# Step sizes in four column strips among the convolution tiles, running sums spread from rows by row halves, a gate tile ahead of turning x, and a provisional mean

## What is computed

```python
xbc = silu(causal_depthwise_conv(xbc, conv_w, conv_b))      # x, B and C of the state space
xs, bm, cm = split(xbc, [D_SSM, D_SSM + GROUPS * STATE])
dt = softplus(dt_raw + dt_bias)                             # step sizes: 512 tokens x 16 heads
a = -exp(a_log)
# in chunks of 128 tokens (4 chunks), adt = dt * a:
a_cs = cumsum(adt)                                          # running sums
decay = exp(segsum(adt))                                    # exp(a_cs[l] - a_cs[s]) for s <= l
cb = einsum('bclgn,bcsgn->bcgls', cc, bc)
y_diag = einsum('bcgjls,bcsgjp->bclgjp', cb * decay, x * dt)
states = einsum('bcsgn,bcsgjp->bcgjpn', bc, x * dt * decay_to_end)
y = y_diag + y_off + d_skip * x                             # y_off from the state of the chunk before
y_ssm = rms_norm(y * silu(z_ssm), ssm_norm_g)
out = concatenate([y_att, y_ssm]) @ w_out
x = layer_norm(alpha * x + out, ln_g, ln_b)                 # mean, variance, scale, bias
```

## Time and profile before

| what | us |
|---|---|
| median of 3 runs | 1355.4 (1354.19 to 1357.29) |
| the profiled execution | 1354.75 |
| its span, first to last instruction | 1353.0 |
| TensorE busy | 1254.0 (93%) |
| VectorE busy | 625.0 (46%) |
| ScalarE busy | 461.8 (34%) |
| GpSimd busy | 158.7 (12%) |

### The profile page before, as it was taken

One profiled execution on the slowest core, in us unless ns is written; L12 is line 12 of the kernel. 1 busy time (PEld: TensorE's weight loads), 2 busy tenths in 40 slices (PEclk: granted clock), 3 DMA queues, 4 the chain that ended last, 5 costly groups with the idle time before them and its releaser, 6 DMA issues.

```text
span 1353.0 us, 17766 instructions
## 1 busy us (share of the span) xinstructions
PE 1254.0 (93%) x6976; PEld 891.0 (66%) x6976; DVE 625.0 (46%) x1131; ACT 461.8 (34%) x837; POOL 158.7 (12%) x126
## 2 busy tenths in 40 slices
PE   4899989999999889999889699999999999999996
PEld 1667556678887564454444278897556898787883
DVE  1654465554444353311111365324655745858544
ACT  3333236542222321111111251125564345555314
POOL 0200010000000000000000201602402056422000
PEclk9899999999999999999999799999999989999998
DMA  9565251023334369999999913321002312112301
GB/s 352 210 208 190 75 222 68 1 63 93 94 97 152 153 264 392 412 411 412 411 412 409 376 47 93 94 78 63 1 2 65 102 37 63 47 52 89 94 16 62
DMA packets 61633, 219.37 MB, mean 162 GB/s; under 512 B 6368, under 2 KB 6760, under 8 KB 61552
## 3 DMA queue, kind: packets, MB, share of 16 engines
q1 hardware_dynamic: 55440, 198.86, 40.3%
q10 hardware_dynamic: 3664, 10.47, 2.0%
q0 software_dynamic: 2448, 8.91, 1.7%
HBM read 203.52 MB, written 14.70 MB: 161 GB/s over the span
## 4 chain that ended last, share of the span: by engine, by line
PE 78%; DMA 8%; DVE 4%; ACT 4%; issue 4%; POOL 1%; SPq 0%; ACTq 0%; DVEq 0%; POOLq 0%
PE ps L639 12%; PE ps L640 12%; PE ps L641 12%; PE ps L926 6%; PE ps L907 4%; PE ps L735 3%; PE ps L947 3%; PE ps L758 3%; PE ps L745 3%; DMA ring<-in_w_moe 2%; PE ps L680 2%; PE ps L682 2%; PE ps L681 2%; PE ps L706 1%; DMA RG<-expert_rows,small 1%
## 5 line engine op out<-in xcount | busy, mean ns | idle before, releaser
L1615 DVE TENSOR_TENSOR ring_r<-ring,ring_r 128x1024 fp32r<-128x1024 f32 x115 | 145.8, 1271 | 206.3 <-ACT ring_r L1273 205.6
L1273 ACT ACTIVATE ring_r<-ring 128x1024 fp32r<-128x1024 f32 x116 | 121.2, 1053 | 204.4 <-PE ps L641 166.8
L639 PE MATMUL ps<-RB_r,ring_r 128*128 128x512 f32 x320 | 126.9, 396 | 1.1 <-DVE RH L1661 1.1
L641 PE MATMUL ps<-RB_r,ring_r 128*128 128x512 f32 x320 | 124.6, 389 | 0.0
L639 PE MATMUL ps<-RC_r,ring_r 128*128 128x512 f32 x224 | 91.2, 407 | 5.7 <-POOL RD_r L2380 4.7
L640 PE MATMUL ps<-RD_r,ring_r 128*128 128x512 f32 x224 | 88.0, 393 | 0.0
L641 PE MATMUL ps<-RC_r,ring_r 128*128 128x512 f32 x224 | 87.9, 392 | 0.0
L640 PE MATMUL ps<-RG_r,ring_r 128*128 128x512 f32 x208 | 81.1, 390 | 0.0
L926 PE MATMUL ps<-ring,RH 128*64 128x512 f32 x320 | 71.9, 594 | 0.0
L639 PEld LDWEIGHTS ps<-RB_r,ring_r 128*128 128x128 f32 x320 | 60.1, 188 | 16.7 <-issue 4.5
L907 PE MATMUL ps<-RD_r,RC_r 128*128 128x256 f32 x288 | 69.1, 296 | 1.2 <-DVE RD_r L1884 1.2
(11 more groups left out here) (438 smaller groups left out, 2620.3 us busy)
## 6 DMA issues: line engine op xcount, KB each, us to landing
ring<-in_w_moe SPq DMA_DIRECT2D x120, 512.0 KB, 15.6
ring<-in_w_post SPq DMA_DIRECT2D x68, 512.0 KB, 3.6
ring<-in_w_pre SPq DMA_DIRECT2D x48, 512.0 KB, 3.6
RE<-in_w_moe SPq DMA_DIRECT2D x44, 512.0 KB, 15.9
RF<-in_w_moe SPq DMA_DIRECT2D x40, 512.0 KB, 14.7
ring<-in_w_pre SPq DMA_DIRECT2D x16, 1024.0 KB, 7.0
expert_rows<-RD ACTq DMA_DIRECT2D x15, 512.0 KB, 6.9
ring<-in_w_pre SPq DMA_DIRECT2D x3, 2048.0 KB, 16.9
```

Source lines behind the costliest of these rows:

```text
L639: mm(out, part(m)[:, w], xh(k), start=first and k == 0, stop=False)
L641: ins = mm(out, remainder(m)[:, w], xh(k), start=False, stop=last and k == n_k - 1)
L1273: A(part(m), tile, ACT.Copy).then_inc(w_hi, 1)
L1615: v.tensor_tensor(remainder(m), arrival(m)[2], part(m).bitcast(F32), ALU.subtract).then_inc(w_split, 1)
```

## The change

- Step sizes: between convolution tiles 6 and 7, eight matmuls with 32 columns of weights (16 of `wdt`, 16 of zeros, copied into `cpad` during the expert stage) over 512 tokens of RA, in four column strips of one bank; ScalarE copies the bank out; before tile 8 four matmuls with `strip_sum` (16 columns that add the four strips) turn them to tokens. VectorE's and ScalarE's softplus stand in the convolution loop, at i = 9 and 11, and i = 10.
- Gate tile 0 runs directly behind the convolution tiles (bank number `PE_Z0`; the numbers behind it shift by one, so the banks' parities swap), then x is turned.
- Running sums: one matmul for sums, one for totals, two that write the sums as rows (head and chunk on partitions, twice), copied to `cs_rows`. `spread_sums` picks a row with a column of `ident` repeated 128 times, over 64 partitions, alternating between the lower and the upper half and between ps[2] and ps[3]; the semaphore comes once for both.
- GpSimd does skip product and scaling of one chunk ahead of the loop and of the next one at the end of each round.
- The end: a provisional mean from six tiles, summed by TensorE ahead of the last output tile; seven tiles are centred by it while that tile runs; squares go to RB and GpSimd adds seven of them; the mean of what is left, d, is subtracted from eight tiles (six on VectorE, two on GpSimd) and d squared from the variance.

Context lines are left out of the diff, as are renamed semaphores and lines that only moved:

```diff
@@ -205,6 +206,8 @@
+        cs_rows = w_r[:, :, :].rearrange("p k n -> p (k n)")[:, 0:P]
+        adt_all = MASK[:, 192:256]
@@ -614,7 +620,8 @@
-                        pe.wait_ge(ev[e % 2], PE_XT // 2)
+                        b = e - PE_XT - 6
+                        pe.wait_ge(ev[b], (PE_XT + 1 - b) // 2)
@@ -1039,8 +1046,23 @@
+                if i == 7:
+                    for k in range(KT):
+                        g = k % 4
+                        last = mm(ps[0][32 * g:32 * g + 32, :], cpad[:, k, :], xT(k), start=(k < 4), stop=(k >= 4))
+                    last.then_inc(heads_full, 1)
+                if i == 8:
+                    pe.wait_ge(heads_sb, 2)
+                    for t in range(TT):
+                        last = mm(ps[1][:, t * 16:t * 16 + 16], PTB[:, 0, t * P:(t + 1) * P], strip_sum, start=True, stop=True)
+                    last.then_inc(heads_full, 1)
...
+            def gate_tile(i):
+                split_column(z_tile(i), M_Z + i, two(RCr, RDr))
+            gate_tile(0)
+            pe.wait_ge(sp1, 2)
@@ -1051,15 +1073,18 @@
-            pe.wait_ge(w_small, 32)
-            pe.wait_ge(ev[0], PE_XT // 2 + 1)
-            for t in range(TT):
-                for k in range(KT):
-                    last = mm(ps[0][:, t * 16:t * 16 + 16], xT(k)[:, t * P:(t + 1) * P], wdt[:, k, :],
-                              start=(k == 0), stop=(k == KT - 1))
-            last.then_inc(dt_full, 1)
+            pe.wait_ge(ev[1], PE_XT // 2 + 1)
+            pe.wait_ge(ev[0], (PE_XT + 1) // 2 + 1)
+            pe.wait_ge(adt_ok, 1)
+            mm(ps[1][:, 0:64], upper[:, :], adt_all, start=True, stop=True)
+            mm(ps[1][:, 64:128], ones[:, :], adt_all, start=True, stop=True)
+            for s in range(2):
+                last = mm(ps[1][64 * s:64 * s + 64, 128:256], adt_all, upper[:, :], start=True, stop=True)
+            last.then_inc(heads_full, 1)
...
+            pe.wait_ge(ev[0], (PE_BT + 1) // 2)
+            pe.wait_ge(ev[1], PE_BT // 2)
@@ -1067,19 +1092,18 @@
-                for q in qs:
-                    if 4 * c + q >= 2:
-                        pe.wait_ge(dd_ok, 4 * c + q - 1)
-                    for h in range(4):
+                if 4 * c + qs[1] >= 2:
+                    pe.wait_ge(dd_ok, 4 * c + qs[1] - 1)
+                for h in range(4):
+                    for q in qs:
+                        half_rows = slice(64 * (q % 2), 64 * (q % 2) + 64)
+                        row = 64 * (q % 2) + 16 * c + 4 * q + h
...
-                                  adt_t[:, c, 4 * q + h:4 * q + h + 1].to_broadcast([P, P]), upper[:, :],
+                                  ident[half_rows, row:row + 1].to_broadcast([64, P]), cs_rows[half_rows, :],
...
-                    last.then_inc(csb_full, 1)
+                last.then_inc(csb_full, 2)
@@ -1090,19 +1114,11 @@
-            gate_tile(0)
-            pe.wait_ge(ev[0], PE_ZA // 2)
-            pe.wait_ge(ev[1], PE_ZA // 2)
-            pe.wait_ge(adt_ok, 1)
-            for c in range(TT):
-                mm(ps[1][:, c * 16:c * 16 + 16], upper[:, :], adt_t[:, c, :], start=True, stop=True)
...
-            last.then_inc(cs_full, 1)
...
+            pe.wait_ge(cs_ok, 1)
...
-            pe.wait_ge(cs_ok, 1)
+            pe.wait_ge(cs_ok, 2)
@@ -1151,6 +1167,9 @@
+                if i == KT - 1:
+                    pe.wait_ge(rsum_ok, KT - 3)
+                    mm(ps[4][:, :], ones[:, :], SQ[:, 1, :], start=True, stop=True).then_inc(mu_full, 1)
@@ -1166,11 +1185,14 @@
-            pe.wait_ge(rsum_ok, KT - 2)
-            mm(ps[4][:, :], ones[:, :], SQ[:, 1, :], start=True, stop=False)
-            pe.wait_ge(r_ok, KT)
-            mm(ps[4][:, :], ones[:, :], RA[:, KT - 1, :], start=False, stop=True).then_inc(mu_full, 1)
-            stats(ST_VAR, KT, 5)
+            pe.wait_ge(cen_ok, KT - 1)
+            mm(ps[2][:, :], ones[:, :], RC[:, KT - 2, :], start=True, stop=False)
+            pe.wait_ge(sq_used, ST_VAR + KT - 2)
+            mm(ps[5][:, :], ones[:, :], RB[:, 0, :], start=True, stop=False)
+            pe.wait_ge(cen_ok, KT)
+            mm(ps[2][:, :], ones[:, :], RC[:, KT - 1, :], start=False, stop=True).then_inc(mu_full, 1)
+            pe.wait_ge(sq_ready, ST_VAR + KT)
+            mm(ps[5][:, :], ones[:, :], RB[:, KT - 1, :], start=False, stop=True).then_inc(sq_used, 1)
@@ -1494,29 +1516,23 @@
+                    if i == 7:
+                        act.wait_ge(heads_full, 1)
+                        A(PTB[:, 0, :], ps[0][:, :], ACT.Copy).then_inc(heads_sb, 1)
+                    if i == 10:
+                        act.wait_ge(sp1, 2)
+                        link(A(tmp_t[:, :, :], tmp_t[:, :, :], ACT.Exp))
+                        A(aneg, rows[:, R_ALOG:R_ALOG + 16], ACT.Exp)
+                        A(tmp_t[:, :, :], tmp_t[:, :, :], ACT.Ln, bias=ones[:, 0:1]).then_inc(sp2, 1)
...
-                if i == 12:
-                    for j in range(1, 8, 2):
-                        x_turned(j)
...
@@ -1542,8 +1558,16 @@
+            hi(M_Z + 2)
+            gate_out(0)
+            for j in range(1, 8, 2):
+                x_turned(j)
+            evict(PE_BT + 1, ([(b_tok[:, 1, :, :], quad(bank(PE_BT + 1)[:, :]))], 1.0))
+            act.wait_ge(cs_ok, 2)
+            A(sd_t[:, :, :], cs_t[:, :, :], ACT.Exp)
+            A(dec_t[:, :, :], tot_t[:, :, :], ACT.Exp)
+            A(dte_t[:, :, :], tmp_t[:, :, :], ACT.Exp).then_inc(sp2, 1)
...
-            gate_out(0)
@@ -1585,7 +1609,16 @@
-            norm(7, ST_VAR, KT, 5, lambda k: RC[:, k, :], lambda k: act.wait_ge(cen_ok, k + 1), eps2)
+            act.wait_ge(x_lo, 16 + KT)
+            for k in range(KT):
+                act.wait_ge(cen_ok, k + 1)
+                A(RB[:, k, :], RC[:, k, :], ACT.Square).then_inc(sq_ready, 1)
+            act.wait_ge(d_ok, 1)
+            A(SQ[:, 1, :], SQ[:, 0, :], ACT.Square).then_inc(sq_ready, 1)
+            act.wait_ge(sq_used, ST_VAR + KT)
+            act.wait_ge(rinv_used, 7)
+            link(A(RINV[:, :], SQ[:, 1, :], ACT.Ln, bias=eps2))
+            A(RINV[:, :], RINV[:, :], ACT.Exp, scale=-0.5).then_inc(rinv_ok, 1)
@@ -1998,6 +2031,10 @@
+                if p == 5:
+                    dve.wait_ge(w_small, 32)
+                    v.tensor_copy(cpad[:, :, 0:16], wdt[:, :, :])
+                    link(v.tensor_reduce(strip_sum, ident[:, :].rearrange("p (g c) -> p c g", g=4)[:, 0:16, :], AX_X, ALU.add))
@@ -2137,8 +2174,19 @@
+                if i == 9:
+                    dve.wait_ge(heads_full, 2)
+                    link(v.tensor_tensor(dt_t, ps[1][:, 0:64].rearrange("p (t h) -> p t h", t=TT),
+                                         rows[:, R_DTB:R_DTB + 16].unsqueeze(1).to_broadcast([P, TT, 16]), ALU.add))
+                    link(v.scalar_tensor_tensor(tmp_t, dt_t, -1.0, dt_t, ALU.mult, ALU.min))
+                    link(v.tensor_scalar(dt_t, dt_t, 0.0, None, ALU.max))
+                    dve.sem_inc(sp1, 1)
...
-                    x_turned(0)
+                    dve.wait_ge(sp2, 2)
+                    link(v.tensor_tensor(dt_t, dt_t, tmp_t, ALU.add))
+                    link(v.scalar_tensor_tensor(adt_t, dt_t, -1.0, aneg.unsqueeze(1).to_broadcast([P, TT, 16]), ALU.mult,
+                                                ALU.mult))
+                    dve.sem_inc(adt_ok, 1)
@@ -2148,27 +2196,15 @@
-            for i in range(2, 8, 2):
+            for i in range(0, 8, 2):
...
-            dve.wait_ge(dt_full, 1)
...
-            lo(M_Z + 2)
-            dve.wait_ge(cs_full, 1)
+            dve.wait_ge(heads_full, 3)
+            v.tensor_copy(cs_rows, ps[1][:, 128:256]).then_inc(cs_ok, 1)
...
-            dve.wait_ge(sp2, 3)
+            evict(PE_BT, ([(b_tok[:, 0, :, :], quad(bank(PE_BT)[:, :]))], 1.0))
@@ -2279,17 +2317,26 @@
+            def centre(k):
+                v.scalar_tensor_tensor(RC[:, k, :], ps[4][:, :], -1.0 / (D - 2 * P), RA[:, k, :], ALU.mult,
+                                       ALU.add).then_inc(cen_ok, 1)
...
-                if i >= 2:
+                if 2 <= i < KT - 1:
...
+                if i == KT - 1:
+                    dve.wait_ge(mu_full, 1)
+                    for k in range(KT - 1):
+                        centre(k)
@@ -2297,13 +2344,27 @@
-            dve.wait_ge(mu_full, 1)
-            for k in range(KT):
-                v.scalar_tensor_tensor(RC[:, k, :], ps[4][:, :], -1.0 / D, RA[:, k, :], ALU.mult,
-                                       ALU.add).then_inc(cen_ok, 1)
-            dve.wait_ge(cen_ok, KT)
+            centre(KT - 1)
+            dve.wait_ge(mu_full, 2)
+            v.tensor_scalar(SQ[:, 0, :], ps[2][:, :], 1.0 / D, None, ALU.mult).then_inc(d_ok, 1)
+            dve.wait_ge(d_ok, 1)
+            def moved(k):
+                v.tensor_tensor(RC[:, k, :], RC[:, k, :], SQ[:, 0, :], ALU.subtract).then_inc(d_ok, 1)
+            moved(0)
+            dve.wait_ge(sq_ready, ST_VAR + KT + 1)
+            dve.wait_ge(sq_used, ST_VAR + KT - 1)
```

(34 more changed lines are left out.)

46 lines of the change are left out of this document (13 added, 33 removed).

## The result

The changed kernel took 1338.64 us in the median (1337.16 to 1340.17, four runs) and the kernel before 1356.35 beside it (1354.19 to 1358.94): a ratio of 0.987, interval 0.985 to 0.989, 17.7 us less. Forecast were 1335.2 us and a range of 1332.5 to 1342.0. The sign, the place of the gain and most terms held. One term, the spread by row halves, gave 0.52 us each instead of 0.83.

The account below looks back on a forecast made before the run. TensorE, busy 1254 of 1353 us, was taken to bound the kernel. The terms +2.75 - 13.7 - 5.8 - 3.4 sum to -20.2 us, from 1355.4 to 1335.2 us, range 1332.5 to 1342 for 8 in 10.

Parts of the forecast that it names:

- Step sizes: Among convolution tiles: strips 1.9 us plus their turning 0.85 us, +2.75 us there; the old 9.21 us of matmuls removed.
- its own account: Whole kernel: the case that all goes as forecast, 1333 to 1338 us, chance 0.64.
- clock rival: Between gate tiles 0 and 1: the clock falls again in narrow work, 1338.2 us, chance 0.08.
- The new stretch: End of last convolution tile to gate tile 1: 12.65 us against 26.39, -13.7 us.
- hides the last convolution and Silu: Gate tile 0 ahead of turning x: claimed to cover that work, with no size given.
- Spreads: Spreading by row halves: 0.83 us less each; seven outside the new stretch give -5.8 us.
- A step of 0.21 for two matmuls: Attention scores in row halves: 4 records list 0.49 us at 128 columns and 0.70 at 256.
- so the same for halves, 0.49 + 3 x 0.21: Spread by row halves: carries the attention-score step on to 1.12 us, where full rows list 1.95.
- loads go in single file and nothing is gained: Spreads: rival that halves don't overlap, so 6.6 us of eight spreads stay, 1341.8 us; chance 0.13.
- Chunk loop: VectorE and GpSimd load in the loop priced at nothing; 0 to 1.5 us per chunk if cover is gone.
- The rival of a stalled loop: Chunk loop: diagonal blocks wait 1 to 1.5 us for state or scaled x, four times, 1340 us; chance 0.12.
- End: Kernel end: scaling starts at 9.9 us behind the last output tile, not 14.2; -3.4 us (1.5 to 5).

Follow-up runs that it names:

- narrow_steps: Against the changed kernel, step sizes again as 64 matmuls with 16 moving columns, issued between convolution tiles; 1347.00 us, ratio 0.994 to the kernel before.
- gate_behind: Against the changed kernel, gate tile 0 moved back behind turning x, the sums and turning b; 1344.88 us, ratio 0.994 to the kernel before.
- skip_first: Against the changed kernel, GpSimd makes skip products and scalings of all four chunks ahead of the chunk loop; 1350.04 us.
- old_end: Against the changed kernel, the old end put back, without provisional mean or moves; 1341.67 us, ratio 0.991 to the kernel before.
- psum_again: Against the changed kernel, VectorE's six end moves read the correction sum from PSUM, second run of that code; 1337.84 us, ratio 0.986 to the kernel before.

## Why the prediction held, and where not

By the time alone the forecast looks better, and worse, than it was. 1338.64 us lies in the range, but above the 1333 to 1338 that the prediction gave its own account, and beside the 1338.2 of its clock rival. The traces decide: the clock was 1.00 through the whole stretch, and of the 3.1 us by which the span fell short, 2.1 are the seven spreads.

- **Step sizes**, +2.75 against +3.09. The strips took 1.86 us to the next start (1.9 said) and the turning 0.81 (0.85). What was missed is small and of the same kind as in the spread: the first convolution matmul behind each takes 0.33 to 0.34 us to the next start, not 0.23, and the one ahead of the strips 0.31. narrow_steps adds where the gain comes from: of the 10.56 us that the strips save there, 6.8 are the clock. The 1.92 us of the earlier trace rows was a row's own length, and left out what going in and out of strips costs its neighbours.
- **The new stretch**, -13.7 against -13.58. Gate tile 0 took 5.44 as said, turning x 3.49, sums 0.90 instead of 0.7, turning b 0.90 with no wait ahead of it (0.3 said), C times B 0.99, the spread 1.09 instead of 0.88. Misses of 0.20 and 0.21 up and 0.27 down nearly cancel, so that the sum is closer than its terms is luck. One term has the wrong reason: "runs directly behind the convolution tiles, at full clock: 5.44 instead of 7.31". In gate_behind the tile stands behind the short work again and takes 5.57 us with the clock at 1.00, so it keeps the clock without that place; what is gone in both kernels is the long run of 16-column matmuls in which the clock had fallen. What the place gives is the cover, "hides the last convolution and Silu", which was left without a number: 5.2 us in this order.
- **Spreads**, -5.8 against -3.67 for seven. This is the step that failed, and it is a size: 0.52 us each, not 0.83. "A step of 0.21 for two matmuls" was near the pair's 0.22, though the rows behind it compare 128 with 256 columns in the same four records and not two matmuls with four, so no further weight load is in it. What failed is "so the same for halves, 0.49 + 3 x 0.21", which was taken off the time to the next start: the fit was made to how long the rows themselves list. That length did fall by nearly the 0.83, from 1.95 to 1.16 us. But a full-row spread of 1.95 us lets a gate tile start after 1.70, and one in halves of 1.16 only after 1.09, so the step became shorter by 0.61 and not 0.83; and the neighbours' steps took back 0.10 before and 0.02 behind. Seven times 0.52 is 3.7, which leaves nothing to VectorE or GpSimd. That loads go in single file and nothing is gained is refuted by the 0.22 us pair.
- On the two pages of the Trainium skill: the rule in "TensorE: Matmul & The Clock Gate", section LDWEIGHTS, gives as an estimate 16 x 107 ns = 1.71 us for any rows; the spread with full rows (1.70 us) and the one with one half behind the other (1.64) are near it, the one with halves in turn is not (1.09). "TensorEngine Tiling (Array Packing)", Key Properties, has parallel loads in different tiles and a drain at a change of mode; the traces agree with the first by the 0.22 us pair, and the 0.28 us for going in and out would fit the second, but no run tells a drain from another cause.
- **Chunk loop** priced at nothing for VectorE and GpSimd: right. TensorE's rows show no wait between G and Y, and one of 0.31 us just behind Y, as before. The decays of chunk 0 stretched to 3.42 us for two, as the rows had warned, within the slack. The rival of a stalled loop did not come; its place and its mechanism are real (skip_first).
- **End**, -3.4 against -3.3 (+1.19 - 4.49). The scaling was said at 9.9 us behind the tile and came at 9.72, held by the moves, as said: RINV was ready at 8.45 (8.25 said). The loss beside GpSimd is real and falls on two of the moves. The two 512-column records of the provisional mean cost 0.92 us by old_end; the rest of Y to E is the longer wait at 1219.58, which old_end has too (1.25 us).
- **The clock rival**: read as falling only where 16-column matmuls run. It did not fall in the changed kernel's stretch, nor with the gate tile behind turning b again (gate_behind). But narrow_steps, skip_first and psum_again show more cases than the prediction had: it fell in narrow work among full tiles, at 6.8 us, and behind waits of TensorE, one of which (2.05 us at 1240.83) the trace of before has too. The prediction had no term for those.

## What to carry to other kernels

Price a change of tiling mode by the start-to-start times of the group, the step ahead of it and the first one behind it, since a group's own listed length leaves out what its neighbours pay; with 0.28 us per entry and exit against 0.2 us saved per pair, row halves should pay from the second pair on, an estimate from the runs with four and eight pairs. Put full-size work over the chains of other engines before TensorE's short work needs their result: one gate tile covered 4.6 us of waits, and short waits can also cost the clock (5.9 us in skip_first). When a stretch of TensorE's gets shorter, look at what it used to cover on the other engines. Where two engines go through the same buffers in the end of a kernel, let one read PSUM, which gave both their speed back here (1.1 us).

## What the runs showed of the hardware that was not expected

- Entering and leaving row halves costs some 0.28 us once, with four pairs as with eight, 0.10 of it on the step before; eight half-row matmuls that do not alternate cost 0.205 us each, nearly as much as full rows (0.213).
- The granted clock fell to 0.50 within 3 us of the first of 64 narrow matmuls, in the middle of full tiles, and stayed there for 13 us; in the kernel before it fell 4 to 6 us behind the first.
- The same code with the same waits (1.24 and 2.04 us) kept the clock in one profile and lost it in another, at 1.4 us; over all thirteen profiles, with these waits at 0.97 to 1.26 and 2.01 to 2.05 us, five lost it.
- Two VectorE operations with both inputs in SBUF took 1.02 and 1.67 us to the next start while GpSimd worked, and 0.60 once it was done; GpSimd's took 1.72 instead of 1.25. With one of VectorE's inputs from PSUM both went at their own pace.
